# Mixers of a two-block transformer kernel: value products one group later, causal score columns, another order of head norms and weight tiles

## The chip, the cores and the metric

The kernel runs on one core of a Trainium2 chip, as one launch. The metric is the device time of that launch in microseconds. Four engines are named below: TensorE (PE in the profile) multiplies, VectorE (DVE), ScalarE (ACT) and GpSimd (POOL) do the rest, and SyncE (SP) issues the transfers of weights.

## The reference

`x` has 256 tokens of 1024 columns, `mem` 256 of 1024, and all is in 32-bit floats. A first block has two layers, each `x + 0.5 swiglu(rms(x))`, a mixer, a cross attention on `mem`, and a second `x + 0.5 swiglu(rms(x))`; the hidden width is 2816. A second block has two layers of feed-forward, mixer, feed-forward. The mixers differ:

- *even* (layer 0): windowed attention with ALiBi bias and sinks, 8 query heads of 64 on 2 key heads, and 8 heads of stick-breaking attention;
- *odd* (layer 1): attention over dilated windows, 16 heads of 64, with a bias for each head;
- *cross attention*, twice: 4 heads of 256, no bias, queries from `x`, keys and values from `mem`;
- *mix* (second block, twice): differential attention, `softmax(q0 k0) - lambda softmax(q1 k1)` for 8 heads of 2 x 64 with a causal mask; a short causal convolution and 8 mLSTM heads; both results go through an rms norm for each head, and a gated sum of two projections.

In even, odd and cross attention, queries and keys are rms-normalised for each head before the scores ("head norm"):

```python
qa = rms_norm(qa.reshape(b, s, A_KV_HEADS, A_GROUP, HEAD_DIM), q_gain)
s = jnp.where(valid, s + bias, -jnp.inf)
p = jnp.exp(s - m[..., None])
o = jnp.einsum('bnhgqk,bnkhd->bnhgqd', p / denom[..., None], vb)
```

## The kernel before

Activations lie turned over, model columns on the 128 partitions and the 256 tokens along the row. Weights come as one stream of 829 tiles of 128 x 1024 numbers in the order in which they are used. SyncE loads a tile into one of three `raw` buffers; ScalarE rounds it to `w_hi` (L818) and VectorE takes the rest as `w_lo` (L1178), in a ring of six, up to four tiles ahead of TensorE; TensorE adds up three products for each block (L394 is the one line on which every product is recorded). The activation has the same two parts, `a` or `b`.

Every engine runs its own program in order; semaphores join them. Four functions give the order of the mixers' work to all engines alike, as lists of units: `before()` (L283, ahead of the attention), `between()` (L305, ahead of the probabilities of group g), `lstm_between()` (L326, inside lstm head h) and `projection_between()` (L337, behind projection tile k). A unit `w` is a weight tile whose 128 result columns go to `z`; `v` is two tiles that give 256 columns of the values in `v`; `hn` is a head norm of two `z` tiles: ScalarE squares them (L957 to L960, into `hmid` or `sil`), TensorE sums over the head with a matrix of ones (`head_sums`, L570), ScalarE takes the root (L967), VectorE the reciprocal (L1362, or L1359 for the mix mixer) and the scaling (L1368), which for the mix mixer is done by GpSimd (`head_apply`, L1700). `split` and `gated` cut such results into high and low parts.

An attention works in groups: a pair of heads of 64 (even 4 groups, odd 8), a pair of maps of one head (mix 8) or one head of 256 (cross 4). The steps of a group, by engine: TensorE scores into banks 0 to 3 (`scores`, L601), 512 columns for each map, a product for each of two query blocks against all 256 keys; VectorE adds the bias and takes the maximum (`biased`, L1384 to L1404); ScalarE takes the exponentials and their sums (`exps`, L979); VectorE the reciprocals of the sums (L1406); GpSimd multiplies the probabilities by them (L1746, L1760), and in the mix mixer VectorE joins the two maps (`combine`, L1419, L1425); TensorE turns the probabilities over in blocks of 128 (L632), ScalarE copies them to `pt` (`turned`, L998, L1004), TensorE multiplies the values (L645 to L653), and ScalarE and VectorE take the result (`result`, L1006). The order on TensorE is short:

```python
for g in range(len(groups)):
    for u in fill[g]: unit(*u)
    for m in range(n_sets):   # 2 for even and odd, 1 for cross and mix
        ...                   # turn map m over
        if g + 2 < len(groups): scores(g + 2, m_)
    ...                       # values of group g
```

GpSimd also does the mix mixer's convolutions (`conv`, L1719, seven instructions each) between the groups, two in group 1 and one in each later group. A silu on ScalarE (its table load at L1061) follows the last of them, and the lstm heads follow that. The mix mixer's queries are multiplied by 1/8 by VectorE before the attention (`q_scaled`).

## Time and profile before

| | |
|---|---|
| time, median of 3 runs | 2891.16 us (2890.49 to 2894.23) |
| the profiled execution | 2888.11 us, span 2886.3 us |
| mean granted TensorE clock | 0.968 |
| busy: TensorE, its weight loads | 2702.4 us (94%), 2466.4 us (85%) |
| busy: VectorE, ScalarE, GpSimd | 2062.4 us (71%), 1540.0 us (53%), 266.7 us (9%) |
| transfers | 447.21 MB, 155 GB/s on average |

The span from the first to the last instruction, in 40 slices of 72 us each; a digit is the busy share of the slice in tenths (9 is 90% or more), and PEclk is the granted TensorE clock in tenths of full speed:

```
PE   7999789999998898999998999999999989999998
DVE  6777676777777575777776667867777676596776
ACT  5555545556555555555555454655555545455554
POOL 0001000000000101000000161200000004421000
PEclk9999999999999899999999998999999999999999
```

The stages in the trace, in us from the start: feed-forward to 206, even mixer to 352 (its attention to 292, the stick-breaking part to 325), cross attention to 458, feed-forward to 857, odd mixer to 1031 (attention to 1005, then its output product), cross attention to 1138, feed-forward to 1555, mix mixer to 1907 (queries, keys and values to 1629, attention to 1732, lstm heads to 1824, projections), feed-forward to 2310, mix mixer to 2680, feed-forward to the end.

### The profile page before, as it was taken

What the parts mean: (1) busy time and instruction counts of PE and PEld (TensorE: products, weight loads), DVE (VectorE), ACT (ScalarE), POOL (GpSimd) and SP (SyncE); (2) the same over time, 40 slices, a digit from 0 to 9 for tenths busy, and PEclk for the clock granted to TensorE, in tenths of its full rate; (3) what the DMA queues carried; (4) which work ended last, traced back from release to release, by engine and by line L of the source; (5) the groups of instructions that cost most, each with busy time, mean ns of one, the idle gap of its engine ahead of it and who ended that gap; (6) DMA issues with size and microseconds to landing.
All of it is one profiled execution on the core that took longest, in us unless ns stands there. A gap on an engine that the chain in (4) does not pass through costs nothing.

```text
span 2886.3 us, 51932 instructions
## 1 busy us (share of the span) xinstructions
PE 2702.4 (94%) x18422; PEld 2466.4 (85%) x18422; DVE 2062.4 (71%) x3101; ACT 1540.0 (53%) x2592; POOL 266.7 (9%) x285
## 2 busy tenths in 40 slices
PE   7999789999998898999998999999999989999998
PEld 7988788998987698998998887889979988889797
DVE  6777676777777575777776667867777676596776
ACT  5555545556555555555555454655555545455554
POOL 0001000000000101000000161200000004421000
PEclk9999999999999899999999998999999999999999
DMA  6654234665553243555664442445645543424453
GB/s 225 216 168 134 78 119 154 212 216 175 189 167 117 74 147 116 181 184 173 189 190 137 140 146 82 138 139 185 192 142 187 182 141 117 131 95 161 148 184 127
DMA packets 123067, 447.21 MB, mean 155 GB/s; under 512 B 13688, under 2 KB 14712, under 8 KB 122816
## 3 DMA queue, kind: packets, MB, share of 16 engines
q1 hardware_dynamic: 120672, 436.79, 47.1%
q0 software_dynamic: 2272, 8.73, 0.9%
q8 instruction: 84, 1.38, 0.2%
q14 instruction: 39, 0.32, 0.0%
HBM read 444.41 MB, written 1.05 MB: 154 GB/s over the span
## 4 chain that ended last, share of the span: by engine, by line
PE 82%; DVE 10%; ACT 4%; issue 2%; POOL 1%; DMA 1%; DVEq 0%; ACTq 0%; SPq 0%; POOLq 0%
PE bank L394 82%; DVE w_lo L1178 1%; DVE a L1205 1%; DVE rt L1362 1%; DVE mx L1398 1%; ACT w_hi L818 1%; DVE z L1244 1%; DVE score L1397 1%; DVE x L1237 1%; PE bank L632 1%; DVE score L1214 0%; POOL z L1731 0%; ACT v L925 0%; DVE rt L1200 0%; POOL score L1746 0%
## 5 line engine op out<-in xcount | busy, mean ns | idle before, releaser
L394 PE MATMUL bank<-a,w_hi 128*128 128x256 f32 (+1 forms) x4656 | 1236.4, 341 | 56.9 <-DVE a L1205 46.2
L1178 DVE TENSOR_TENSOR w_lo<-raw,w_hi 128x1024 fp32r<-128x1024 f32 x829 | 1002.2, 1230 | 282.5 <-ACT w_hi L818 282.0
L394 PEld LDWEIGHTS bank<-a,w_hi 128*128 128x128 f32 x4656 | 799.6, 194 | 147.7 <-issue 38.3
L394 PE MATMUL bank<-a,w_lo 128*128 128x256 f32 x3384 | 916.9, 284 | 0.1
L818 ACT CAST w_hi<-raw 128x1024 fp32r<-128x1024 f32 x829 | 843.6, 1047 | 105.9 <-DMA raw<-in_stream_dram 92.8
L394 PEld LDWEIGHTS bank<-a,w_lo 128*128 128x128 f32 x3384 | 652.6, 193 | 18.4 <-DVE a L1205 0.9
L394 PE MATMUL bank<-b,w_hi 128*128 128x256 f32 (+1 forms) x1984 | 493.4, 330 | 13.5 <-DVE z L1610 6.5
L394 PE MATMUL bank<-h_hi,w_hi 128*128 128x256 f32 x1408 | 394.8, 280 | 4.2 <-DVE h_lo L1178 3.6
L394 PE MATMUL bank<-h_hi,w_lo 128*128 128x256 f32 x1408 | 394.8, 280 | 0.0
L394 PE MATMUL bank<-h_lo,w_hi 128*128 128x256 f32 x1408 | 394.4, 280 | 0.0
L394 PEld LDWEIGHTS bank<-b,w_hi 128*128 128x128 f32 x1984 | 334.4, 193 | 47.7 <-issue 8.1
L394 PE MATMUL bank<-b,w_lo 128*128 128x256 f32 x1344 | 365.7, 283 | 0.1
L394 PEld LDWEIGHTS bank<-h_lo,w_hi 128*128 128x128 f32 x1408 | 265.4, 188 | 7.5
L394 PEld LDWEIGHTS bank<-h_hi,w_hi 128*128 128x128 f32 x1408 | 264.3, 188 | 5.9 <-issue 5.9
L394 PEld LDWEIGHTS bank<-h_hi,w_lo 128*128 128x128 f32 x1408 | 265.1, 188 | 0.0
L394 PEld LDWEIGHTS bank<-b,w_lo 128*128 128x128 f32 x1344 | 257.5, 192 | 6.2 <-DVE b L1205 0.4
L866 ACT COPY pt<-bank 128x256 f32<-128x256 f32 x176 | 65.8, 374 | 224.6 <-PE bank L394 224.4
L870 ACT CAST h_hi<-hmid 128x256 fp32r<-128x256 f32 x176 | 71.4, 406 | 194.7 <-DVE hmid L1273 194.7
L862 ACT COPY pt<-bank 128x256 f32<-128x256 f32 x176 | 65.4, 371 | 203.2 <-PE bank L394 203.1
L1680 POOL TENSOR_TENSOR score<-score 128x256 f32<-128x256 f32 x48 | 43.7, 911 | 1353.4 <-ACT score L846 1352.3
L394 PE MATMUL bank<-w_hi,a 128*128 128x256 f32 x736 | 134.8, 285 | 0.0
L1178 DVE TENSOR_TENSOR h_lo<-hmid,h_hi 128x256 fp32r<-128x256 f32 x176 | 74.9, 426 | 83.0 <-ACT h_hi L870 83.0
(186 smaller groups left out, 2873.1 us busy)
## 6 DMA issues: line engine op xcount, KB each, us to landing
raw<-in_stream_dram SPq DMA_DIRECT2D x829, 512.0 KB, 4.0
z<-in_biasc_dram POOLq DMA_DIRECT2D x8, 512.0 KB, 5.8
z<-in_biasa_dram POOLq DMA_DIRECT2D x4, 512.0 KB, 5.1
x<-in_x_dram SPq DMA_DIRECT2D x1, 1024.0 KB, 6.2
v<-in_mem_dram POOLq DMA_DIRECT2D x2, 512.0 KB, 6.5
out_dram<-x SPq DMA_DIRECT2D x8, 128.0 KB, 1.8
con<-in_con_dram POOLq DMA_DIRECT2D x1, 896.0 KB, 5.2
vec<-in_vec_dram POOLq DMA_DIRECT2D x1, 421.0 KB, 6.9
```

The costliest lines, as they stand in the source:

```text
L394: return nc.tensor.matmul(out, lhsT, rhs, start=start, stop=stop, skip_group_check=shared)
L632: last = nc.tensor.transpose(out[:, col:col + P], p[:, qb * T + kb * P:qb * T + kb * P + P], ident)
L818: nc.scalar.copy(w_hi[:, slot, :], raw[:, raw_slot, :]).then_inc(hi_split, 1)
L862: nc.scalar.copy(pt[:, jj, 0:T], bank[4 + 2 * jj][:, T:2 * T]).then_inc(gate_rest, 1)
L866: nc.scalar.copy(pt[:, jj, T:2 * T], bank[5 + 2 * jj][:, T:2 * T]).then_inc(up_rest, 1)
L870: nc.scalar.copy(h_hi[:, jj, :], hmid[:, jj, :]).then_inc(hhi_done, 1)
L1178: return nc.vector.tensor_tensor(out, a, hi.bitcast(F32), ALU.subtract)
L1205: nc.vector.scalar_tensor_tensor(lo[:, c, :], source, gain(name, c), hi[:, c, :].bitcast(F32), ALU.mult, ALU.subtract).then_inc(signal, 1)
L1237: nc.vector.tensor_tensor(x[:, c, :], temp[:, c, :], x[:, c, :], ALU.add).then_inc(x_ready, 1)
L1244: nc.vector.scalar_tensor_tensor(temp[:, c, :], source(c), gain(name, c), r, ALU.mult, ALU.mult)\
L1362: chain(nc.vector.reciprocal(r, r))
L1680: ins = nc.gpsimd.tensor_tensor(sq[:, 0, :], sq[:, 0, :], sq[:, c, :], ALU.add)
```

## The change

1. *Scores.* Even, odd and mix compute 384 columns for each map in place of 512: the first query block against its own 128 keys, the second against 256. The products of the two maps of a group, which use the upper and the lower 64 rows of the array, follow each other by turns. Bias tables and the causal mask shrink to match.
2. *Softmax.* VectorE adds the bias and takes the negated maximum in one `tensor_tensor_reduce` for each query block; the factor 1/8 of the mix mixer goes into it. In cross attention the copy of the scores goes: maximum and exponentials read the bank. The reciprocals of both maps are one instruction, ahead of the next group's bias. GpSimd's normalisation is two instructions (128 and 256 columns) in place of one.
3. *Values.* TensorE computes the values of group g - 1 ahead of turning over group g, and the scores of g + 2 stand between the two turn-overs. ScalarE does the units of the group ahead of the copies, and the result after the first copy.
4. *Head norms.* The squares (`hs`) are issued on their own, one tile or more before the sum, root and scaling (`hn`), and for the mix mixer the multiplication by the gain too.
5. *Order.* The odd mixer takes all q and k tiles before the attention; the values' tiles are spread over the groups, one (`vh`, a half of `v`) in each. Cross attention takes all keys but the last norm before it. Norms in the lstm heads move from heads 1, 3 and 5 to 1, 2 and 6, those in the projections from k = 1 to k = 2, and the gated parts from 5 and 6 to 4 and 5. Each convolution but the last stands in the group after its own number, the last one behind the attention.

```diff
-            first = bias_tile[kind] + 2 * i
-            return z[:, first:first + 2, :].rearrange("p a t -> p (a t)")
+            first = bias_tile[kind]
+            return z[:, first:first + (12 if kind == "even" else 24), :].rearrange("p a t -> p (a t)")[:, 384 * i:384 * i + 384]
+        def spans(kind):
+            return ((0, T), (T, 2 * T)) if kind == "xa" else ((0, P), (P, 3 * P))
...
         def before(kind, layer):
+            def hs(name, i, a, b):
+                return ("hs", name, i, layer, a, b)
             def hn(name, i, a, b):
                 return ("hn", name, i, layer, a, b)
...
             if kind == "even":
+                return [("first", "a", "x", 0), w(1), w(2), ("col", "x"), hs("evq", 0, 0, 1), w(3), w(4),
+                        hs("evq", 1, 2, 3), hn("evq", 0, 0, 1), ("v", "a", "x", v, 0), hs("evk", 0, 4, 4),
+                        hn("evq", 1, 2, 3), ("v", "a", "x", v, 1), hn("evk", 0, 4, 4), ("v", "a", "x", v, 2)]
             if kind == "odd":
+                out = [("first", "a", "x", 0), w(1), w(8), ("col", "x"), hs("odq", 0, 0, 1), w(9)]
+                for i in range(4):
+                    q, k = (2 * i, 2 * i + 1), (2 * i + 8, 2 * i + 9)
+                    nq, nk = (2 * i + 2, 2 * i + 3), (2 * i + 10, 2 * i + 11)
+                    if i < 3:
+                        out += [w(nq[0]), hs("odk", i, *k), hn("odq", i, *q), w(nq[1]), w(nk[0]), hs("odq", i + 1, *nq),
+                                hn("odk", i, *k), w(nk[1])]
+                    else:
+                        out += [("vh", "a", "x", v, 0, 0), hs("odk", i, *k), hn("odq", i, *q)]
+                return out
             if kind == "xa":
...
+                return [("first", "a", "x", 8), w(9), ("mem",), w(10), hq(hs, 0), w(11), ("stat", "m"), w(12), hq(hs, 1),
+                        hq(hn, 0), w(13), ("col", "m"), w(14), hq(hs, 2), hq(hn, 1), w(15), k(0), hq(hs, 3), hq(hn, 2),
+                        k(1), k(2), hk(hs, 0), hq(hn, 3), k(3), k(4), hk(hs, 1), hk(hn, 0), k(5), k(6), hk(hs, 2),
+                        hk(hn, 1), k(7), hk(hn, 2)]
...
             if kind == "even":
                 return [[("w", "a", "x", 5 + 2 * g), ("w", "a", "x", 6 + 2 * g)] for g in range(4)]
             if kind == "odd":
+                last = ("hn", "odk", 3, layer, 14, 15)
+                return [[("vh", "a", "x", v, (g + 1) // 2, (g + 1) % 2)] + ([last] if g == 0 else []) for g in range(7)] + [[]]
             if kind == "xa":
+                k3 = ("xak", 3, layer, 6, 7)
+                return [[("hs", *k3), ("v", "b", "m", v, 0), ("hn", *k3)]] + [[("v", "b", "m", v, g)] for g in range(1, 4)]
...
             out = [("w", "a", "x", 32 + 2 * h), ("w", "a", "x", 33 + 2 * h)]
-            if h in (1, 3):
-                out += [("hn", "diff", i, layer, 2 * i, 2 * i + 1) for i in (h - 1, h)]
-            if h in (2, 4):
-                out += [("split", h - 2), ("split", h - 1)]
-            if h == 5:
-                out += [("hn", "lstm", i, layer, 8 + 2 * i, 9 + 2 * i) for i in (0, 1)]
-            return out
+            return out + {0: [diff("hs", 0), diff("hs", 1)],
+                          1: [diff("hn", 0), diff("hn", 1), diff("hs", 2), diff("hs", 3)],
+                          2: [diff("hn", 2), diff("hn", 3), ("split", 0), ("split", 1)],
+                          3: [("split", 2), ("split", 3)],
+                          4: [long("hs", 0)],
+                          5: [long("hs", 1)],
+                          6: [long("hn", 0), long("hn", 1)],
+                          7: []}[h]
...
-            if k == 1:
-                return [("gated", 1)] + [("hn", "lstm", i, layer, 8 + 2 * i, 9 + 2 * i) for i in (2, 3)]
-            return [("gated", {0: 0, 5: 2, 6: 3}[k])] if k in (0, 5, 6) else []
+            return {0: [("gated", 0), long("hs", 2)], 1: [("gated", 1), long("hs", 3)], 2: [long("hn", 2), long("hn", 3)],
+                    4: [("gated", 2)], 5: [("gated", 3)]}.get(k, [])
+        def hn_banks(name, i):
+            if (name, i) == ("odk", 3):
+                return (6,)
+            return {"diff": (6,), "lstm": (6,), "xaq": (1, 3), "xak": (1, 3)}.get(name, (2, 3))
...
-                if name in ("odq", "odk") and o_read[0]:
-                    pe.wait_ge(o_lo, o_read[0])
...
+                def scores(g):
...
+                        s = exp_done if kind == "xa" else max_done
+                        pe.wait_ge(s, base[s] + nm * (g - 1))
+                    for b, (lo, hi) in enumerate(spans(kind)):
+                        for e in range(len(maps[0][0])):
+                            for m, (qs, ks, part, _) in enumerate(maps):
+                                last = mm(bank[2 * (g % 2) + m][:, lo:hi], z[part, qs[e], b * P:(b + 1) * P],
+                                          z[part, ks[e], 0:hi - lo], e == 0, e == len(qs) - 1)
+                                if b == 1 and e == len(qs) - 1:
+                                    last.then_inc(s_mm, 1)
+                def values(g):
+                    if g >= 1:
+                        s = o_out if kind == "mix" else o_lo
+                        pe.wait_ge(s, base[s] + g)
+                    if kind == "odd" and g == 0:
+                        pe.wait_ge(hroot, t.so_far(hroot))
+                    if kind in ("odd", "xa"):
+                        pe.wait_ge(v_ready, v_of[g // 2 if kind == "odd" else g])
+                    pe.wait_ge(pt_ready, base[pt_ready] + n_sets * (g + 1))
+                    outs = groups[g]["outs"]
+                    order = [(kb, o) for o in outs for kb in range(2)] if kind == "xa" else [(kb, o) for kb in range(2) for o in outs]
+                    for kb, (m, vc, width, row, col) in order:
+                        p = pt[:, (n_sets * g + m) % 2, :]
+                        out = bank[O_BANK][row:row + width, col:col + T]
+                        first = P if kb and blocks == 1 else 0
+                        last = mm(out[:, first:T], v[:, kb, vc:vc + width], p[:, kb * T:kb * T + T - first],
+                                  kb == 0, kb == 1, True)
+                    last.then_inc(o_done, 1)
...
+                scores(0)
+                scores(1)
                 for g in range(len(groups)):
                     for u in fill[g]:
                         unit(*u)
                     if g >= 1:
+                        values(g - 1)
+                    turn_over(g, 0)
+                    if g + 2 < len(groups):
+                        scores(g + 2)
+                    if n_sets == 2:
+                        turn_over(g, 1)
+                values(last_group)
...
                     unit(*u)
-                pe.wait_ge(v_ready, t.so_far(v_ready))
                 if kind == "even":
                     pe.wait_ge(qk_ready, t.so_far(qk_ready))
+                    pe.wait_ge(v_ready, v_of[0])
                 elif kind == "mix":
-                    pe.wait_ge(q_scaled, t.next(q_scaled))
+                    pe.wait_ge(v_ready, t.so_far(v_ready))
...
                 def exps(g):
+                    if g >= 2:
+                        act.wait_ge(recip_done, base[recip_done] + g - 1)
-                        if g >= 2:
-                            act.wait_ge(recip_done, base[recip_done] + nm * (g - 2) + m + 1)
+                        for b, (lo, hi) in enumerate(spans(kind)):
+                            p = score[:, g % 2, m, lo:hi]
+                            source, sign = (bank[2 * (g % 2)][:, lo:hi], 1.0) if kind == "xa" else (p, -1.0)
+                            last = nc.scalar.activation(p, source, ACT.Exp, bias=nmx[:, k, b:b + 1], scale=sign,
                                                         accum_out=rs[:, k, b:b + 1])
...
                 for g in range(len(groups)):
                     if g + 1 < len(groups):
                         exps(g + 1)
+                    for u in fill[g]:
+                        unit(*u)
+                    turned(g, 0)
                     if g >= 1:
                         result(g - 1)
-                    for u in fill[g]:
-                        unit(*u)
-                    turned(g)
+                    if n_sets == 2:
+                        turned(g, 1)
...
+                        if kind == "xa":
+                            chain(nc.vector.tensor_reduce(mx[:, k, :], src.rearrange("p (b n) -> p b n", b=2), AX.X, ALU.max))
+                            nc.vector.tensor_scalar(nmx[:, k, :], mx[:, k, :], -1.0, None, ALU.mult).then_inc(max_done, 1)
+                            continue
-                        src = bank[2 * (g % 2) + m][:, :]
-                        if kind == "xa":
-                            chain(nc.vector.tensor_copy(s, src))
-                        else:
-                            chain(nc.vector.tensor_tensor(s, src, bias_of(kind, head), ALU.add))
-                        chain(nc.vector.tensor_reduce(mx[:, k, :], s.rearrange("p (b n) -> p b n", b=2), AX.X, ALU.max))
-                        if kind == "even":
-                            last = nc.vector.tensor_scalar(nmx[:, k, :], mx[:, k, :], gain("sinks", head), -1.0,
-                                                           ALU.max, ALU.mult)
-                        else:
-                            last = nc.vector.tensor_scalar(nmx[:, k, :], mx[:, k, :], -1.0, None, ALU.mult)
+                        for b, (lo, hi) in enumerate(spans(kind)):
+                            last = nc.vector.tensor_tensor_reduce(
+                                score[:, g % 2, m, lo:hi], src[:, lo:hi], bias_of(kind, head)[:, lo:hi],
+                                -(HD ** -0.5) if kind == "mix" else -1.0,
+                                nsink[:, head:head + 1] if kind == "even" else -FAR, ALU.add, ALU.min, nmx[:, k, b:b + 1])
+                            if b == 0:
+                                last.then_inc(dve_step, 1)
+                                t.next(dve_step)
                         last.then_inc(max_done, 1)
                 def reciprocals(g):
-                    for m in range(nm):
-                        k = 2 * (g % 2) + m
-                        dve.wait_ge(exp_done, base[exp_done] + nm * g + m + 1)
-                        if kind == "even":
-                            chain(nc.vector.tensor_tensor(rs[:, k, :], rs[:, k, :], es[:, k, :], ALU.add))
-                        if kind == "mix" and m == 1:
+                    dve.wait_ge(exp_done, base[exp_done] + nm * (g + 1))
+                    sums, out = rs[:, k:k + nm, :], rr[:, k:k + nm, :]
+                    if kind == "even":
+                        chain(nc.vector.tensor_tensor(sums, sums, es[:, k:k + nm, :], ALU.add))
+                    last = nc.vector.reciprocal(out, sums)
+                    if kind == "mix":
+                        chain(last)
+                        last = nc.vector.tensor_scalar(rr[:, k + 1, :], rr[:, k + 1, :], lam[:, 5:6], None, ALU.mult)
+                    last.then_inc(recip_done, 1)
...
                 biased(0)
                 for g in range(len(groups)):
+                    reciprocals(g)
                     if g + 1 < len(groups):
                         biased(g + 1)
-                    reciprocals(g)
-                    if kind != "mix" and g >= 1:
-                        result(g - 1)
+                    if kind != "mix" and g >= 1:
+                        result(g - 1)
...
-                        dve.wait_ge(w_evac, t.so_far(w_evac))
-                        nc.vector.tensor_scalar(z[:, 0:8, :], z[:, 0:8, :], HD ** -0.5, None, ALU.mult)\
-                            .then_inc(q_scaled, 1)
...
+            def head_gain(name, i, layer, a, b):
+                pool.wait_ge(hsq, hs_count[0])
+                for e, tile in enumerate((a, b)):
+                    nc.gpsimd.tensor_scalar(z[:, tile, :], z[:, tile, :], gains[e], 1.0, ALU.mult, ALU.mult)\
+                        .then_inc(pool_step, 1)
...
+                def normalised(g, m):
+                    k = 2 * (g % 2) + m
+                    for b, (lo, hi) in enumerate(spans(kind)):
+                        p = score[:, g % 2, m, lo:hi]
+                        last = nc.gpsimd.tensor_scalar(p, p, rr[:, k, b:b + 1], 1.0, ALU.mult, ALU.mult)
+                        if b == 0:
+                            last.then_inc(pool_step, 1)
+                            t.next(pool_step)
+                    return last
                 for g in range(len(groups)):
-                        nc.gpsimd.tensor_tensor(p, p, rr[:, k, :].unsqueeze(2).to_broadcast([P, 2, T]), ALU.mult)\
-                            .then_inc(a_part, 1)
-                        if g == 1:
-                            conv(layer, 0)
+                        normalised(g, 1).then_inc(a_part, 1)
                         if g >= 1:
-                            conv(layer, g)
+                            conv(layer, g - 1)
+                if kind == "mix":
+                    conv(layer, 7)
```

## Rows read from the trace of the kernel before

**Rows 1.** Table of stretches; us from:to and length, busy of each engine, clock, DMA, GB/s.

```profile
205.70:291.90 86.20, 77.00 (x558) 67.46 (x558) 63.88 (x103) 48.73 (x102) 10.51 (x11) 1.00 0.40 128
...
352.00:458.20 106.20, 94.12 (x673) 88.53 (x672) 72.48 (x98) 56.56 (x97) 7.50 (x7) 0.98 0.37 119
...
857.30:1004.60 147.30, 123.52 (x777) 101.09 (x777) 104.67 (x155) 85.50 (x165) 18.68 (x19) 0.88 0.28 93
...
1629.00:1732.30 103.30, 91.05 (x701) 84.87 (x701) 70.11 (x128) 54.47 (x116) 62.16 (x64) 0.96 0.40 127
...
1732.30:1823.90 91.60, 86.30 (x525) 74.04 (x525) 74.91 (x93) 49.51 (x67) 13.30 (x18) 0.92 0.26 81
...
1823.90:1853.80 29.90, 25.36 (x184) 23.86 (x185) 24.95 (x26) 20.12 (x29) 14.27 (x10) 0.94 0.47 150
```

**Rows 2.** Chain of waits, 1560 to 1630; start, us, step.

```profile
1560.80 67.23 PE bank L394 x556
```

**Rows 3.** Waits of TensorE, whole trace: releaser, us in all, times, longest.

```profile
PE bank L632 <- DVE score L1425: 12.0, 5, 4.6
...
PE bank L394 <- ACT pt L1004: 6.9, 8, 1.1
...
PE bank L394 <- DVE z L1610: 6.5, 2, 3.2
...
PE bank L394 <- ACT sil L960: 4.9, 3, 1.7
```

**Rows 4.** Waits of TensorE in the odd mixer, 857.3 to 1004.6.

```profile
PE bank L394 <- ACT hmid L960: 9.6, 3, 6.3
```

**Rows 5.** Waits of TensorE in the first cross attention, 352 to 458.3.

```profile
PE bank L394 <- ACT hmid L960: 4.3, 3, 2.1
```

**Rows 6.** Waits of TensorE in the even mixer, 205.7 to 291.9.

```profile
PE bank L394 <- ACT hmid L958: 1.7, 1, 1.7
...
PE bank L394 <- ACT v L925: 0.9, 1, 0.9
```

**Rows 7.** Timeline of TensorE, attention products: start, us, instructions, wait before.

```profile
259.43 1.13 PE L394 MATMUL bank<-z 64*128 64x256 f32 x4
...
262.74 0.88 PE L394 MATMUL bank<-pt,v 128*64 128x256 f32 x8
...
280.67 1.50 PE L394 MATMUL bank<-pt,v 128*64 128x256 f32 x8
...
291.98 2.99 PE L394 MATMUL bank<-z 64*128 64x256 f32 x32 [0.92 <-DVE b L1178]
...
1639.24 1.14 PE L394 MATMUL bank<-z 64*128 64x256 f32 x8
```

**Rows 8.** Groups of VectorE by form; busy, mean ns, idle before.

```profile
L1362 DVE RECIPROCAL rt<-rt 128x512 f32<-128x512 f32 x8 | 26.8, 3351 | 9.9 <-ACT rt L967 9.9
...
L1397 DVE TENSOR_TENSOR score<-bank,z 128x512 f32<-128x512 f32 x16 | 11.0, 687 | 6.9 <-PE bank L394 6.9
...
L1398 DVE TENSOR_REDUCE mx<-score 128x2 f32<-128x512 f32 x16 | 11.0, 686 | 0.5
...
L1541 DVE SCALAR_TENSOR_TENSOR score<-bank,gcol,con 128x128 f32<-128x128 f32 x8 | 2.7, 342 | 0.0
```

**Rows 9.** Timeline of GpSimd and ScalarE, end of the first mix attention.

```profile
1726.27 0.72 POOL L1731 TENSOR_TENSOR z<-z 128x253 f32<-128x253 f32 x1
...
1728.94 1.28 ACT L1061 ACT_TABLE_LOAD   x1
```

**Rows 10.** Timeline of VectorE and ScalarE, projections of the first mix mixer.

```profile
1837.04 6.56 DVE L1359 RECIPROCAL rt<-rt 128x512 f32<-128x512 f32 x2
...
1848.07 0.62 ACT L943 CAST a<-z 128x512 fp32r<-128x512 f32 x1 [6.56 <-POOL z L1698]
```

**Rows 11.** Groups of GpSimd by form, convolution steps.

```profile
L1729 POOL TENSOR_SCALAR z<-z,vec 128x255 f32<-128x255 f32 x8 | 11.6, 1451 | 0.7
...
L1729 POOL TENSOR_SCALAR z<-z,vec 128x253 f32<-128x253 f32 x8 | 3.9, 482 | 0.8
```

280 lines of the change are left out of this document (124 added, 156 removed).

## The prediction

> **What bounds the kernel now.** First the slices of the page: TensorE is busy for nine tenths or more in most of them, and the lower ones are those of the mixers. Then the table of stretches, which puts the idle time there in numbers. A reader subtracts PE busy from the length of each stretch: even mixer 86.2 - 77.0 = 9.2 us, cross attention 12.1 (there are two alike), odd mixer 23.8, attention of the first mix mixer 12.3, its lstm heads 5.3 and projections 4.5 [rows 1]. The granted clock is the second loss: a mean of 0.88 over the 147.3 us of the odd mixer means about 35 us at 1.2 GHz; in the even and cross stretches it stays at 2.4 GHz or nearly [rows 1]. Next the chain: 23 weight tiles in a row take 67.2 us, 2.9 us a tile, with nothing between them [rows 2]. So TensorE sets the pace and each tile costs 2.9 us; the change keeps every weight tile, and can win only waits, half-clock time and attention products. Last the waits of TensorE say who ends them: VectorE's combination behind GpSimd in the mix mixers, 12.0 for both; the copy of turned-over columns; a late projection result; and squares for head norms, the `sil` and `hmid` lines [rows 3], of which 9.6 lie in the odd mixer [rows 4], 4.3 in each cross attention [rows 5] and 1.7 in the even one [rows 6].
>
> **The change, part by part.** All durations are from one execution of 2888.1 us (span 2886.3).
>
> *Products.* In even and odd groups one map's scores took 1.06 us from start to next start (x4, 259.43), so 2.12 for a pair; the values of a pair took 0.8 when both copies were there (262.74) and 1.4 when the second came late (280.67). Where heads of the two array halves follow each other, 16 products with 3072 columns took 2.99 us (291.98) [rows 7]: 1 ns a column, and a pair of 768 columns would take about 0.7. I take 0.7 for scores and 0.7 for values. Bounds for scores: 0.7, and 768 columns at the 259.43 rate (512 in 1.06), 1.6. Saved: 2 even groups x 1.4, 6 odd groups x 1.4, and 0.5 for each first pair of groups; mix, whose pair already took 1.07 (1639.24), 0.35 x 8 x 2.
>
> *Softmax on VectorE.* A map costs 0.69 (bias) + 0.69 (maximum) [rows 8] and a small sign change, about 1.5 us. Afterwards two fused instructions of 128 and 256 columns. No row shows one; below, two plain ones give 0.76 (0.34 for 128 columns, and 0.42 for 256, between that and 0.69 for 512) [rows 8]; above, no faster than now, 1.5. I take 0.85, nearest to the plain ones, since bias and maximum take the same time each, so both go by columns. TensorE doesn't wait for this in steady state, so it is worth nothing itself; it shortens the first group of each attention.
>
> The Trainium skill ("VectorE: DVE Perf Modes", "Two Vector instructions with no wait between them") says that an op that also writes out its accumulator is two instructions. With two reads, priced by me as small as the sign change (0.15, an estimate), a map would cost about 1.1, and the sum would be the same. No run so far shows it.
>
> *Even mixer.* The two waits for squares (1.7, and 1.4 of the 4.9 on `sil`) [rows 3, 6], with 0.2 for each restart, go: the squares are now issued a tile earlier. The wait for the last v copy goes (0.9). But ScalarE now does both groups' exps, later because VectorE's second bias waits for the first reciprocals, and then two 1.04 splits before the first copy of turned-over columns; I put that wait of TensorE at 2.4, against about 1.7 of waits there now, part of the stretch's 9.2 [rows 1, 6]. Scores 2.8 + 0.5, values 1.2 (1.4 to 0.8 twice), minus 0.7 for the last group, where nothing covers the copy. Sum: 3.5 + 0.9 - 0.7 + 3.3 + 0.5 = 7.5, **7 saved** (3 to 10).
>
> *Cross attention, twice.* Waits for squares 4.3 + 1.7, four of them, with 0.35 restart each, and one of two copy waits, 1.06 + 0.3, go [rows 3, 5]; about 4 us of other waits stay. A wait is added: before the first scores TensorE now waits for the root of the last key pair, 1.1. Sum: 6.0 + 1.4 + 1.3 - 1.1 = 7.6, **15 for both** (9 to 18). The first probabilities are covered by the v product, two tiles of 2.9.
>
> *Odd mixer.* I measure from the first head norm at 874.0 to 1004.6, 130.5 us. New order: 19 of the tiles 55, head sums 4, eight pairs of scores 5.6, sixteen turn-overs 7, eight values 5.6: 77. Then the waits. (1) All q and k tiles now come first, and a pair of tiles costs VectorE one reciprocal of 3.35 [rows 8], two splits, two results and two scalings, 7.2 in all, TensorE 6.3. Seven pairs: VectorE is the bound, and TensorE waits about 7. (2) Root before the first scores, 1. (3) Start-up: TensorE waits about 3 for the first probabilities, because VectorE still scales the last queries; then 3.8 for the first copy, since ScalarE, in order, first does the exps of group 1, a split and the last root with its 1.28 table load [rows 9]; 0.7 and 3.1 in group 1 for the same queue. From group 2 on a group is one 2.9 tile + 0.7 + 0.7 + 0.84 = 5.2 to 5.5, and ScalarE (2 x 0.9 of exps, split 1.0, copies 0.8, v 0.4, result 0.3: 4.3) and VectorE (3.2) fit in. (4) Last two groups 2.2. (5) Output wait 1.3 as now, and one tile more before the first head norm, 2.4. Total 77 + 7 + 1 + 10.6 + 2.2 + 3.7 = 101.5, so 29 less; I give 5 back for half-clock stretches after the start-up waits (now 35 us, of which I take 26 as with work, 13 lost) [rows 1]. **24 saved** (10 to 38, the ends being start-up and phase one twice as bad, or hidden).
>
> *Mix attention, twice.* The waits for the combination go, 6.7 of the 12.0 in the first, 4.6 the longest [rows 3]: one convolution now stands ahead of a normalisation where two stood. After the 4.6 wait TensorE ran at half clock, 8 us in this stretch by the mean of 0.96 [rows 1]; I take 2.7 as lost. One copy wait 0.7, scores 2.8 [rows 3, 7]. **13 each, 26.** Given back: GpSimd is busy 62.2 in this stretch [rows 1]; less eight normalisations of 1.04 that is 6.7 a convolution, 7.4 with its gaps. Before, the last one ended at 1727.0 and ScalarE began the silu's table load at 1728.9 [rows 9]. Now two follow the last normalisation, 15 to 16 us, while TensorE has 12.5 left: **+3 each, 6** (0 to 10).
>
> *Lstm heads.* VectorE is busy 74.9 of 91.6 us [rows 1], close behind TensorE; the 2 x 3.28 of reciprocals per pair of norms isn't removed but moved (heads 1, 3, 5 become 1, 2, 6). Squares early take 0.6 off each second head sum, but the single bank keeps the root between them. **0** (3 either way each).
>
> *Projections, twice.* The norms move from k=1 to k=2 and the gated parts from 5 and 6 to 4 and 5. VectorE reached the reciprocals at 1837.0, TensorE waited 3.2 for the result of tile 3, and ScalarE stood 6.6 before gated part 2 [rows 3, 10]. In the new order VectorE first waits for the split that ScalarE issues after a sigmoid table load, so reciprocals start 4 us later; TensorE then waits about 5 for the result of tile 4 and, since ScalarE stands before gated part 2 with tile 9 unsplit, about 4 more for tile 5. 11 against 5 now, with half clock behind it: **+7 each, 14** (0 to 20).
>
> The bias transfers (12 pieces to 9), the constants and the extra tiny op run beside feed-forward tiles: nothing. q_scaled's 1.2 us on VectorE had cover too.
>
> Sum: -7 - 15 - 24 - 26 + 6 + 14 = -52. 2888.1 - 52 = 2836; the median of the runs is 3.1 above the profiled one, so **2839**.
>
> **Rivals.** *A, the give-backs are hidden* (projections, silu, half the start-up): -52 - 14 - 6 - 7 = -79, 2812. For it: they are predicted waits in queues that I followed, and TensorE has four tiles split ahead. Against: the 3.2 wait exists already [rows 3].
> *B, the odd mixer is bound by VectorE and half clock*: saving 10 there, 3 in even and 10 in cross, rest as forecast: -29, 2862. For it: with a wait of 6.3 in it [rows 4] this stretch had a mean clock of 0.88 [rows 1].
> *C, slower*: VectorE's queue in the mix mixers. Norm pairs now stand at heads 1 and 2, one behind the other, then at 6 and at k=2. If each pair's 6.6 us lies bare instead of beside tiles, that is 4 x 6.6 x 2 = 52 in place of the 14, with 20 of half clock: -66 + 52 + 20 = +6, 2897. It decides when VectorE enters head 1 already late. Against: at heads 1, 3, 5 tiles covered all but a little, since TensorE is idle only 5.3 us in the stretch [rows 1].
> *D, GpSimd locked out.* A convolution step of 255 columns takes 1.45 on average, one of 253 0.48 [rows 11]: something holds GpSimd for about an instruction of VectorE. Normalisations are now twice as many instructions; if each waited 1.0, an odd group's four would take 6.3 against a slack of 2, 8 x 1.5 us in odd, 4 us in each mix: -52 + 12 + 8, 2859. The Trainium skill ("SBUF — State Buffer", "SBUF: two separate sides") has the rule: a VectorE instruction with two SBUF inputs and a GpSimd one exclude each other for their whole length; the split has two, the fused softmax one. The 1.45 agrees. Against D: normalisations stand where VectorE mostly waits or reads PSUM.
>
> **Numbers.** Forecast 0.50 (own range 2822 to 2855), A 0.24, B 0.12, D 0.06, C 0.05, the rest 0.03. 2803 to 2868 holds 8 in 10. Runs agree within about 0.1%, so 0.2% (6 us) can be told: faster 0.93, same 0.02, slower 0.05.
>
> **What would show it.** Head sums in the odd mixer without ScalarE ahead of them and VectorE busy over 90% until the first scores; groups of 5.5 us from the third on; two convolutions after the last normalisation and a longer wait before the silu; two waits of 4 to 5 us in the projections where one of 3.2 stood; score pairs of 0.7. Wrong if pairs take 1.4 or more, if the fused instruction takes over 0.9 for 256 columns, or if the projections don't lengthen.

## The result, and the profile after

The changed kernel takes **2827.4 us** (median of 4 runs, 2827.0 to 2828.1) against 2890.9: a ratio of 0.9778, interval 0.9761 to 0.9795. It is 63.5 us faster; 52 were forecast (2839, range 2803 to 2868). The profiled execution took 2827.0 us, span 2825.2. From the page:

```profile
span 2825.2 us, 51938 instructions
...
PE 2670.6 (95%) x18422; PEld 2448.2 (87%) x18422; DVE 2006.6 (71%) x3116; ACT 1512.7 (54%) x2578; POOL 246.5 (9%) x330
```

TensorE is busy 31.8 us less and its idle time fell by 29.3 (183.9 to 154.6). The record of the granted clock divides the busy time further: if what lies in stretches at 1.2 GHz is counted at half, TensorE's work fell from 2631.1 to 2611.2 us, and what half clock adds to it from 71.3 to 59.4. So of the 61.1 us between the two profiled executions 29.3 are waits, 19.9 fewer or better overlapping products, and 11.9 half clock. This measure of work is steady: it is 2631.0 to 2631.2 in the three kernels with the old products (before, 6 and 9 below) and 2610 to 2613 in all but one of those with the new ones.

The stretches that answer to [rows 1], cut at the same instructions of TensorE, with the same columns:

```profile
205.60:283.23 77.63, 71.79 (x558) 64.33 (x559) 56.37 (x103) 47.58 (x102) 9.85 (x19) 1.00 0.42 142
344.77:444.76 99.99, 92.94 (x673) 88.26 (x672) 70.70 (x94) 54.15 (x95) 9.08 (x11) 0.98 0.39 127
843.89:965.64 121.75, 105.72 (x778) 89.77 (x778) 89.21 (x163) 73.11 (x157) 15.34 (x35) 0.96 0.34 113
...
1585.45:1676.40 90.95, 86.24 (x702) 81.85 (x701) 56.33 (x136) 51.82 (x116) 54.63 (x72) 1.00 0.44 144
1676.40:1768.35 91.95, 84.92 (x525) 72.88 (x524) 76.16 (x93) 48.21 (x66) 13.68 (x19) 0.93 0.26 81
1768.35:1801.25 32.90, 26.36 (x185) 24.46 (x185) 23.12 (x24) 18.21 (x26) 13.39 (x10) 0.90 0.36 119
```

| stretch, us | before | after | difference | forecast |
|---|---|---|---|---|
| even mixer's attention, and the stick-breaking part behind it | 86.3 + 33.2 | 77.6 + 34.6 | -7.2 | -7 |
| cross attention, two | 106.1, 106.3 | 100.0, 100.2 | -12.2 | -15 |
| odd mixer, and its output product | 147.5 + 26.8 | 121.8 + 28.3 | -24.2 | -24 |
| mix attention, two | 103.6, 104.0 | 90.9, 90.6 | -26.0 | -26 + 6 |
| lstm heads, two | 91.3, 91.3 | 92.0, 91.8 | +1.2 | 0 |
| projections, two | 29.7, 29.9 | 32.9, 34.1 | +7.4 | +14 |
| the rest, with what follows the last product | | | 0.0 | 0 |
| profiled executions | 2888.1 | 2827.0 | -61.1 | -52 |

Waits of TensorE over the whole trace, those that answer to [rows 3]:

```profile
PE bank L418 <- DVE z L1664: 11.6, 4, 4.7
...
PE bank L681 <- ACT pt L1059: 10.6, 7, 4.2
...
PE bank L681 <- POOL score L1809: 2.4, 1, 2.4
```

The wait for the combination (12.0) and the waits for squares (`sil`, `hmid`) are gone. Those for squares in the lstm heads and projections (`score`, eight of 1.3 us before) became waits for the root (`rt`, eight of 0.87 to 1.02). The projection wait (`z`, 6.5 before) has grown to 11.6, the wait for copies (`pt`) from 6.9 to 10.6.

**Product pairs and the fused instruction**, timeline of TensorE in a steady odd group, then VectorE's groups in the odd mixer:

```profile
936.57 0.93 PE L418 MATMUL bank<-z 64*128 64x128 f32 x8
...
940.77 0.87 PE L418 MATMUL bank<-pt,v 128*64 128x256 f32 x8
```

```profile
L1457 DVE CUSTOM_DVE_ANT_0 score<-bank,z 128x256 f32<-128x256 f32 x16 | 6.7, 419 | 0.0
...
L1457 DVE CUSTOM_DVE_ANT_0 score<-bank,z 128x128 f32<-128x128 f32 x16 | 4.4, 274 | 0.0
...
L1457 DVE DVE_READ_ACCUMULATOR2_ANT nmx<- 128x1 f32 x32 | 2.6, 83 | 0.0
```

Start to next start a pair of scores takes 0.86 us and a pair of value products 0.80 (0.7 forecast for each). A map (two fused instructions, each with a read of its accumulator) costs VectorE 0.42 + 0.27 + 2 x 0.08 = 0.86 us; 0.85 was taken. The rule of the Trainium skill holds ("VectorE: DVE Perf Modes", "Two Vector instructions with no wait between them"): the op that writes its accumulator is two instructions in the trace. The read is 0.08 us, less than the 0.15 estimated for it.

### The profile page after: what moved, and what is told of

Read it like the earlier page. It is cut to its first block, busy times and chain, and to the rows that moved or that the text cites. A ratio compares the mean times of both kernels' runs of the same rounds, so it can differ in the third digit from the quotient of the medians.

```text
span 2825.2 us, 51938 instructions
## 1 busy us (share of the span) xinstructions
PE 2670.6 (95%) x18422; PEld 2448.2 (87%) x18422; DVE 2006.6 (71%) x3116; ACT 1512.7 (54%) x2578; POOL 246.5 (9%) x330
## 4 chain that ended last, share of the span: by engine, by line
PE 84%; DVE 9%; ACT 4%; issue 2%; DMA 0%; POOL 0%; DVEq 0%; ACTq 0%; SPq 0%; POOLq 0%
PE bank L418 84%; DVE w_lo L1235 1%; DVE rt L1422 1%; DVE a L1262 1%; DVE z L1301 1%; PE bank L681 1%; ACT w_hi L862 1%; DVE x L1294 1%; ACT score L1047 1%; DVE rt L1419 0%; DVE score L1271 0%; DVE rt L1257 0%; DVE z L1381 0%; ACT rt L1021 0%; DVE b L1262 0%
## 5 line engine op out<-in xcount | busy, mean ns | idle before, releaser
L418 PE MATMUL bank<-b,w_hi 128*128 128x256 f32 (+1 forms) x1984 | 492.2, 329 | 20.3 <-DVE z L1664 11.6
L418 PEld LDWEIGHTS bank<-b,w_hi 128*128 128x128 f32 x1984 | 333.6, 193 | 55.8 <-DVE z L1664 12.7
```

The costliest lines, as they stand in the source:

```text
L418: return nc.tensor.matmul(out, lhsT, rhs, start=start, stop=stop, skip_group_check=shared)
```

## The experiments

Each kernel was run five times (5 four times, 9 eleven times); medians are set against 2827.4 for the changed kernel, or 2890.9 where the kernel before is the base. The kernel before was timed again beside each set of runs, with medians of 2890.4 to 2891.0; the changed kernel was not. Stretches are of one profiled execution each, again cut at the same instructions of TensorE.

**1. Old order in the projections.** `projection_between` as before:

```diff
+ 0: [gated 0], 1: [gated 1, hs 2, hn 2, hs 3, hn 3], 5: [gated 2], 6: [gated 3]
```

> The changed kernel with the old order in the projections alone: both norms of lstm heads behind projection tile 1, squares right ahead of their sums, gated parts behind tiles 5 and 6. Theory (the order costs what the changed kernel lost there): the two projection stretches go back from 32.9 and 34.1 us to 29.8 each, 7.5 us less in all, 2820 us. TensorE then waits once for 3.2 us instead of 4.7 and 0.7. Rival (the loss comes from what precedes, VectorE entering the projections later because the norms moved to head 6): the stretches keep 33 or more, 2827.

Measured: **2820.8** (ratio to before 0.9744 to 0.9771), 6.6 less. The stretches are 29.7 and 30.6, against 29.7 and 29.9 in the kernel before. The waits of TensorE in the first, then those of the changed kernel:

```profile
PE bank L418 <- DVE z L1664: 3.2, 1, 3.2
PE bank L418 <- DVE z L1381: 2.1, 1, 2.1
PE bank L418 <- ACT score L1009: 1.3, 1, 1.3
```

```profile
PE bank L418 <- DVE z L1664: 5.5, 2, 4.7
PE bank L418 <- DVE z L1381: 2.1, 1, 2.1
PE bank L418 <- ACT rt L1021: 1.0, 1, 1.0
```

The new order is what costs there; the saved wait for squares (1.3 to 1.0) is less than the longer wait for a result. This part of the change is a loss. 11 and 12, which hold the old order too, have the first stretch at 29.7 as well.

**2. The two norms apart.** `1: [gated 1, hs 3, hn 2], 2: [hn 3]`, the rest as changed.

> The changed kernel with the first of the two norms in the projections (sum, root, reciprocal) behind tile 1 and the second behind tile 2; squares stay a tile early, gated parts at 4 and 5. Theory (the 4.7 us wait is the two reciprocals of 3.28 us in a row on VectorE, ahead of a result): each reciprocal then stands beside one tile of 2.9 us, the wait falls to 1 to 2 us and the stretches to 29 to 31 us: 3 to 9 us less in all, 2819 to 2824. Rival (ScalarE's order with its table loads sets it): within 1 us of the changed kernel.

Measured: **2822.3**, stretches 30.6 and 32.1. Three waits of 0.9, 1.5 and 2.9 us stand where one of 4.7 and one of 0.7 stood: better than both norms at tile 2, not better than the old order.

**3. Values in their own group.** `values(g)` behind turning over group g in place of `values(g - 1)` ahead of it.

> The changed kernel with the value products of group g behind turning over group g again, all else as changed. Theory: in even and odd groups TensorE waits 0.66 us for the last copy in each of the 11 groups where a tile covered it, about 8 us; in the mix mixers the scores of 0.86 cover the copy of 0.48 but for 0.3, 14 times 0.3 = 4; cross attention nothing. 12 us slower, 2839. Rival: the order of values is worth only what the last groups show (1 to 3 us), because scores and turn-overs cover the copies as before; 2829.

Measured: **2845.6**, 18.2 more. Even +2.2, odd +3.3, mix +1.5 each: 8.5 in all, 12 forecast. Cross attention, where nothing was expected, is 5.2 and 5.5 longer. TensorE's waits in the first:

```profile
PE bank L418 <- DVE a L1233: 4.8, 3, 2.2
```

The changed kernel has 1.9 there. ScalarE and VectorE take the result of group g - 1 behind the copy of group g, so values(g) finds its bank unread and waits 2.2, twice. These waits are 2.9 of the 5.2 us; half clock adds 1.3 (7 us of it in the stretch in place of 3). Over the whole kernel the waits for a copy ahead of value products (`pt`) are 7.7 us in thirteen, in place of 2.0 in three. The two moves (values, and the place of the result on ScalarE) belong together; this kernel shows the price of one alone.

**4. Scores map by map.** 384 columns, both products of one map and then both of the other.

> The changed kernel with 384 columns as changed, but the two products of one map and then the two of the other, not by turns. Theory 1 (products follow each other at once only when neighbours use different halves of the array; the lone map's 512 columns took 1.06): a pair takes 1.6 us in place of 0.86, 26 later pairs and four first ones of two, about 34 times 0.7: 24 us slower, 2851. Theory 2 (the pair of the mix mixer, which before stood by map and took 1.07 for 1024 columns, shows that one neighbouring change of halves in a pair is enough): 0.9 us for a pair, 1 to 3 us slower, 2829.

Measured: **2826.8**, no difference; a pair takes 0.86 either way. Theory 2 holds. What makes a pair fast is that the second map stands right behind the first (one map alone took 1.06 for 512 columns in [rows 7]), not that the maps alternate block by block.

**5. Softmax in plain instructions.**

```diff
-last = nc.vector.tensor_tensor_reduce(s, src, bias, factor, sink, ALU.add, ALU.min, low)
+chain(nc.vector.scalar_tensor_tensor(s, src, factor, bias, ALU.mult, ALU.subtract))
+last = nc.vector.tensor_reduce(low, s, AX.X, ALU.min)
```

> The changed kernel with the fused bias-and-maximum (0.27 and 0.42 us for 128 and 256 columns, and 0.08 each for the accumulator, 0.86 a map) taken apart into a plain instruction and a reduction for each block, about 1.4 us a map; same columns, same order. Theory: VectorE has slack in the groups, so only the first probabilities of the four attentions come later, by 0.5 to 1 us each: 2 to 4 us slower, 2831. Rival: the order of the odd mixer has made VectorE's time in the attention count (reciprocal, two maps and a split in each group), every one of its groups grows by 1.1 us: 10 us slower, 2838.

Measured: **2851.1**, 23.7 more. In the profiled execution, 26.0 longer, the odd mixer has +9.3, even +5.5 and each mix attention +3.6, 22 in all; over the whole kernel TensorE's idle time is 17.8 more, half clock adds 8.1 more, and its work is the same. Both theories were too low, the rival nearer. The waits of TensorE in the odd mixer of this kernel, then of the changed one:

```profile
PE bank L681 <- ACT pt L1059: 13.7, 8, 5.3
PE bank L681 <- POOL score L1813: 3.6, 1, 3.6
```

```profile
PE bank L681 <- ACT pt L1059: 7.6, 4, 4.2
PE bank L681 <- POOL score L1809: 2.4, 1, 2.4
```

ScalarE shows why, in a steady odd group of the plain kernel:

```profile
942.43 0.40 ACT L1047 ACTIVATE score<-score,nmx 128x128 f32<-128x128 f32 x1 [1.50 <-DVE nmx L1461]
...
943.67 0.40 ACT L1047 ACTIVATE score<-score,nmx 128x128 f32<-128x128 f32 x1 [0.26 <-DVE nmx L1461]
...
944.57 1.03 ACT L862 CAST w_hi<-raw 128x1024 fp32r<-128x1024 f32 x1
945.50 0.82 ACT L972 ACTIVATE v<-bank,rcol_x 128x256 f32<-128x256 f32 x2
946.22 0.47 ACT L1059 COPY pt<-bank 128x384 f32<-128x384 f32 x1
```

ScalarE stands for VectorE's minimum, and the split, the v columns and the copy that TensorE waits for are queued behind its exponentials. VectorE has idle time, but how long its softmax takes is on the loop: groups take 6.9 and 5.7 us by turns in place of 5.5.

**6. The fused instruction alone, in the kernel before** (blocks of 256 columns in even, odd and mix).

> The kernel before with the fused bias-and-maximum alone (two instructions of 256 columns and their accumulators, about 1.0 us a map in place of 1.55), in even, odd and mix; nothing else. Theory: in the kernel before TensorE's groups are longer and wait for squares and the combination, not for the softmax: 2 to 6 us less, 2887, against 24 us in the changed kernel, where the group is as short as the chain of softmax steps. Rival: the fused instruction is worth about as much here as there (0.55 us x 56 maps, 20 us or more less), 2870.

Measured: **2867.9** (ratio 0.9905 to 0.9932), 23.0 less than before. The theory falls: the instruction is worth about as much there. The profiled execution, at 2862.9 the fastest of the five, has odd -6.1, mix attention -5.1 and -7.0 and even -2.0, 20 us in the stretches that hold the instruction (22 in 5); the lstm heads and projections behind the first mix attention, whose work is unchanged, have another -3.9. Half of the gain is clock: idle time is 12.5 less, and half clock adds 12.8 less. In the odd mixer TensorE's wait for squares fell from 9.6 to 5.2, likely because VectorE, which writes the results that are squared, spends less on the maxima ahead of them; the wait for scaled queries and keys rose from 6.8 to 8.8. In the first mix attention TensorE's wait for the combination, 6.7 before (of the 12.0 in [rows 3]), is 2.4, though the convolutions stand as before:

```profile
PE bank L633 <- DVE score L1430: 2.4, 1, 2.4
```

**7. Two convolutions in group 1**, none behind the attention.

> The changed kernel with GpSimd's convolutions as before, two in group 1 of the mix attention and one in each later group, none behind the attention. Theory: GpSimd's two convolutions (some 14 us) again hold back the normalisation of group 2, now against a shorter group of 8 us: TensorE waits 5 to 6 us in each mix attention, with half clock behind it; both stretches 5 to 8 us longer, 2837 to 2843. Nothing comes back at the end, since the wait for the silu is 3.6 us in both kernels. Rival: GpSimd's convolution got faster with the order of VectorE's work and the wait is gone anyway; 2828.

Measured: **2833.1**, 5.7 more; in the profiled execution the two attentions are 2.3 and 2.1 longer, with one wait of 1.8 and one of 1.4 for the combination. Direction as expected, size a third: what was put down to GpSimd alone was in good part VectorE's softmax ahead of the combination (6). That execution took 2829.6, only 2.6 more than the changed kernel's: half clock adds 1.4 less in it, in stretches whose work is unchanged. So of the 5.7 us between the medians the traces bear out 4.4, and the rest is within what unchanged work moves by.

**8. Squares late.** Every `hs` right ahead of its `hn`.

> The changed kernel with all squares (and the gain multiplications) right ahead of their own sums again. Theory: a wait of TensorE for a result and its square, about 1.3 us, comes back at every head norm that stands right behind the tile it needs: even 3, cross attention 6 each, odd 7 (VectorE sets the pace there with 7.1 us for a pair of tiles and TensorE's slack is only 0.24), some 22 us slower, 2849. Rival: in the odd mixer VectorE hides it, and only even and cross lose, 12 us slower, 2839.

Measured: **2840.1**, 12.7 more: the rival's number. Even +3.5, cross attention +3.2 and +3.4, the lstm heads and projections +2.3 in all, odd mixer +1.1 (and -1.5 in its output product, whose work is the same, with the clock). In the odd mixer's first phase a pair of tiles takes 7.1 us as in the changed kernel: VectorE sets the pace there and early squares gain nothing. At the start of the attention they do count: the last norm's sum now waits 7.4 us for its squares, but in place of waits of 2.4 for the first probabilities and 4.2 for the first copy, so that little is left of it. In the first cross attention only one wait for squares comes back, of 1.4.

**9. The odd mixer's order alone, in the kernel before.**

> The kernel before with one part of the change: all q and k tiles of the odd mixer ahead of the attention, the values' tiles two by two in groups 0, 2, 4 and 6; squares, products, columns and the place of the values stay as before, one bank for the head sums. Theory: of the 24 us that the changed kernel saves in this mixer the order itself gives about 10 (the 9.6 us of waits for squares shrink only in part), 8 come from products side by side and 7 from early squares: 2881. Rival: the order is the whole of it (half-clock time goes with the waits): 2868. Other rival: it gains nothing without the others, since groups without a tile leave the copies bare: 2891 or more.

Measured: **2893.2** (ratio 1.0006 to 1.0024), 2 slower: the second rival. The odd stretch is 3.5 longer. This kernel, to be set beside the odd row of [rows 1]:

```profile
858.93:1009.90 150.97, 131.40 (x777) 104.92 (x778) 104.63 (x155) 75.68 (x157) 18.67 (x19) 0.85 0.28 91
```

Its waits of TensorE in this stretch:

```profile
PE bank L635 <- POOL score L1760: 6.5, 3, 2.4
PE bank L397 <- ACT hmid L963: 4.7, 1, 4.7
PE bank L397 <- DVE z L1327: 4.3, 5, 3.3
```

TensorE's idle time fell from 23.8 to 19.6 us, but its busy time rose from 123.5 to 131.4 for the same products: the mean clock went from 0.88 to 0.85, and the record of the clock has 44 us at 1.2 GHz here, 34 before, 10 in the changed kernel. With half-clock time counted at half, the work is 110.3 and 110.4. The order took 4.2 us of waits away, and the products lost 7.9 to the clock: TensorE was busy in 26 of the 34 us at 1.2 GHz before, and in 42 of the 44 here.

**10. The values' tiles by twos** in the changed kernel: `[vh, vh, hn], [], [vh, vh], [], [vh, vh], [], [vh], []`.

> The changed kernel with the values' half tiles of the odd mixer in twos: two each ahead of groups 0, 2 and 4, one ahead of group 6, none ahead of 1, 3, 5 and 7; all else as changed. Theory (a tile in each group covers the chain of reciprocals, maxima, exponentials and copies, about 4 to 4.5 us a group, against 2.6 us of TensorE's own work there): two groups take about 12.6 us in place of 10.96, some 6 us more in the mixer, 2833. Rival: the queues run ahead and only the sum of the two groups counts: 2827. Other rival: bare groups cost as in the kernel with the order alone, over 12 us: 2840 or more.

Measured: **2832.3**; but the odd mixer and its output are only 0.8 longer in sum (124.1 + 26.8 against 121.8 + 28.3), and 2.3 for the mixer alone. The rival for the mixer: queues run ahead over two groups. The other 4.8 us between the profiled executions lie in unchanged work: mix mixers' lstm heads and projections +2.0, feed-forward +2.3, cross attention +0.6. So groups without a tile cost little by themselves in the changed kernel; why they wait 2.4 us each for probabilities in 9 was not taken apart further.

**11 and 12. The last norm ahead of group 3 (with 1's order), and the first copy first.**

```diff
+([last] if g == 3 else [])          # 11 and 12
+if kind == "odd" and g == 0: turned(g, 0)   # 12: ahead of the units of group 0
```

> The changed kernel with the old order of the projections, and the odd mixer's last norm (its sum, root, reciprocal of 3.35 us, scaling, and two table loads of 1.28 on ScalarE) ahead of group 3 instead of group 0. Theory: of TensorE's 4.2 us wait for the first copy 2.0 go, and most of the 2.1 in group 1; in group 3 ScalarE gets 3.3 us more against 1.2 of slack, 2 us back: 1 to 3 us less in the odd mixer, beside the 6.6 of the projections, 2818. Rival: in the steady groups the norm costs as much or more than at the start: odd mixer within 1 us or longer, 2821 to 2824.

> The kernel before this one (old order of the projections, last norm ahead of group 3), and ScalarE does the first copy of turned-over columns of the odd mixer ahead of the split and the v columns of group 0. Theory: the copy comes 1.9 us earlier and TensorE's wait there goes to about 0.5; 1 to 2 us less in the mixer than without it, 2817. Rival: ScalarE's sum of work in groups 0 and 1 is the bound, the wait only moves to group 1: no difference, 2818.

Measured: **2823.2** and **2819.9** (0.9741 to 0.9768), against 2820.8 for 1 alone. In 11 the odd mixer is 2.5 longer than in the changed kernel and its output product 1.5 shorter with the clock: its rival. The waits of 4.2 for the first copy and 2.1 in group 1 became one of 1.1; but the wait for the first probabilities is 0.8 longer, and in the steady groups, where the norm now stands, there are two new ones of 1.8 and 2.9. In 12 the mixer is 1.0 shorter than in the changed kernel (its output again 1.5), and the wait of 1.1 is gone. 12 has the lowest median; it can't be told from 1, but every run of both lies below the lowest of the changed kernel (2825.3 and 2822.5 at most, against 2827.0).

## Why the prediction was right, and where it was not

- *Total.* Right, with 9 us of the 61 between the profiled executions not foreseen: 6.6 at the projections and 6 at the silu, against 3 too many at cross attention and 1 at the lstm heads. Part of this is luck, as the next three points show: the odd mixer's number has two errors that cancel, and the softmax had no price of its own.
- *Odd mixer*: -24 forecast, -24.2 measured. The pace of the first phase was right: a pair of tiles takes 7.1 us (7.2, VectorE's sum). The 7 us of TensorE's waits booked there were not: they came to 0.9, because TensorE's own work for a pair is 6.9 us (two tiles 5.9, the head's sum 1.0), not 6.3. Score and value pairs at 0.86 and 0.80 in place of 0.7 add 2. From the first norm on TensorE waited 14.7 us in place of the 22 of the sum, and worked 84 us (half clock counted at half) in place of 77: two errors that cancel. The waits of the start-up came nearer: 1.5 for the root (1), 2.4 for the first probabilities (3), 4.2 for the first copy (3.8), 2.1 in group 1 (0.7 + 3.1), 2.6 in the last two groups (2.2) and 1.0 at the output (1.3). Steady groups: 5.5 us (5.2 to 5.5). Half clock fell from 34 to 10 us, and TensorE's work in the stretch by 8.3 us, which no experiment undid.
- *Softmax*: the price was right (0.86), the step "TensorE doesn't wait for this in steady state, so it is worth nothing itself" was wrong. Undoing it costs 23.7 (5), and alone in the kernel before it gives 23.0 (6). The forecast survived because its groups of 5.5 us already took 0.85 a map for granted; the credit went to products, order and convolutions. The forecast's reason (ScalarE 4.3 and VectorE 3.2 fit into 5.5) counted busy time and left out that maximum, exponentials, split and copy follow each other.
- *Mix attention*: -13 each, measured -12.6 and -13.4, by parts other than named: convolutions 2, softmax 4, values 1.5 (experiments 7, 5, 3), and 2.5 of TensorE's own work for scores and values. The rest is not told apart; that the 13 came out so closely is luck.
- *Silu*: no give-back where 3 each were forecast. The last two convolutions took 12.4 us (1661.1 to 1673.5), not 15 to 16, and ended beside ScalarE's table load:

```profile
1672.49 1.28 ACT L1118 ACT_TABLE_LOAD   x1
1672.75 0.72 POOL L1794 TENSOR_TENSOR z<-z 128x253 f32<-128x253 f32 x1
```

  TensorE's wait for the silu is 3.6 us in both kernels.
- *Projections*: +7 each forecast, +3.2 and +4.2 measured. The first wait was right (5, measured 4.7); the second (4, for tile 5) was 0.7 in the first mixer and 1.4 in the second. ScalarE did stand before gated part 2, for 9.8 us (6.6 before), but TensorE went on with tiles already split: the mis-sized term is what that stand costs TensorE.
- *Cross attention*: -7.6 each, measured -6.1. Early squares give 3.3 (8), not 6.0: with late squares only one of the four waits of before comes back, so the others went with another part of the change. The keys' tiles, now all ahead of the attention, are the likely one, but that order was not undone alone.
- *Rival A* came in part: the silu's give-back was hidden, that of the projections by half, that of the start-up not. *Rival D*: an odd group's four normalisations took 1.6 us, not 6.3; they find GpSimd's way free. The lock-out that it fears does occur, in each cross attention once, where a normalisation took 2.5 us. *Rival B* had the right mechanism for another kernel: it is what happened to the order alone (9). *C* did not come: the lstm heads took 0.6 more each.

Undoings of softmax, values, squares and convolutions cost 23.7 + 18.2 + 12.7 + 5.7 = 60.3 us. They overlap, so they are prices of taking one part away, not shares of the 63.5: the 19.9 us of TensorE's own work stand beside them. Two parts were never undone in the changed kernel: the smaller columns, and the order of the odd mixer and of cross attention.

## What to carry to other kernels

Slack in an engine's busy time does not show that its instruction is off the path: follow one group around all engines, and ask what is queued behind the instruction that waits for it. A new order that removes waits need not pay by itself: here it took 4.2 us of waits out of the odd mixer and lost 7.9 to half clock; price it together with the instructions on its loop. When several moves go in at once, undo each alone: here the projections' new order was a loss of some 7 us inside a gain of 2%.

## What the runs showed of the hardware

- Two score products of the same map and two of the other cost the same as four alternating ones, 0.86 us for 768 columns.
- Unchanged work takes 1 to 2 us more or less from kernel to kernel with the clock. The stick-breaking part is the same in the changed kernel and in 4:

```profile
283.23:317.81 34.58, 19.23 (x112) 16.08 (x113) 23.93 (x36) 18.18 (x23) 0.00 (x0) 0.71 0.00 0
```

```profile
283.37:316.66 33.29, 18.73 (x113) 16.12 (x113) 24.03 (x36) 18.18 (x23) 0.00 (x0) 0.74 0.00 0
```

  So single stretches are compared here with that margin. Over a whole kernel it adds up to 5 us (10 above), and differences of totals below that are read only where a stretch of the trace bears them out.
- A convolution step of GpSimd that meets a split of VectorE takes 1.56 us, the same step with VectorE idle 0.48 (timeline of the changed kernel, end of the first mix attention):

```profile
1666.40 1.56 POOL L1792 TENSOR_SCALAR z<-z,vec 128x253 f32<-128x253 f32 x1
1666.48 1.22 DVE L1235 TENSOR_TENSOR w_lo<-raw,w_hi 128x1024 fp32r<-128x1024 f32 x1
...
1672.19 0.48 POOL L1792 TENSOR_SCALAR z<-z,vec 128x253 f32<-128x253 f32 x1
```

  That agrees with the Trainium skill ("SBUF — State Buffer", "SBUF: two separate sides"), by which one of the two excludes the other. VectorE pays as well, when GpSimd's step is further ahead:

```profile
1661.84 0.54 POOL L1792 TENSOR_SCALAR z<-z,vec 128x255 f32<-128x255 f32 x1
1662.11 1.34 DVE L1235 TENSOR_TENSOR w_lo<-raw,w_hi 128x1024 fp32r<-128x1024 f32 x1
```

  Here the split takes 1.34 in place of 1.22, and GpSimd's step its usual time. In the rows above GpSimd's step had started first too, but only 0.08 us earlier, and it was the one held. The same section gives the way to whichever starts first. By the starts recorded in the traces of before and after, that holds for all 15 steps of GpSimd that began 0.2 to 0.5 us ahead of a split (they took 0.37 to 0.54 us), but of 21 that began at most 0.1 us ahead 18 were held (1.5 to 1.6 us).

  These rows also correct how [rows 11] were read: the long form there is not the slow one by itself; after the change the 128x253 form is the slow one (1.33 on average) and the 128x255 form the quick one (0.62).
